# The factors of the x rows travel as a ninth column of the running sums

## What is computed

```python
def rms_norm(x, g):
    y = xf * lax.rsqrt(jnp.mean(xf * xf, axis=-1, keepdims=True) + EPS)
    return (y * g.astype(jnp.float32)).astype(x.dtype)

h = rms_norm(x, norm1_g)
proj = h @ w_in.astype(h.dtype)
...
a_cs = jnp.cumsum(a_dt, axis=-1)
seg = a_cs[..., :, None] - a_cs[..., None, :]
decay = jnp.where(mask, jnp.exp(jnp.where(mask, seg, 0.0)), 0.0)
```

## Time and profile before

| | us |
|---|---|
| median of 3 runs | 2737.02 |
| the runs | 2734.02, 2737.02, 2743.93 |
| the profiled execution | 2734.35 |
| its span, first to last instruction | 2732.5 |

### The profile page before, as it was taken

The page is one execution under the profiler, slowest core; times in us unless marked ns, Lnnn a source line. Parts: engine busy times, 40 slices in busy tenths (PEclk is TensorE's granted clock), DMA queues, the critical chain, the costliest instruction groups (busy, mean ns, idle before and its releaser), DMA issues.

```text
span 2732.5 us, 38705 instructions
## 1 busy us (share of the span) xinstructions
PE 2691.0 (98%) x11487; PEld 1741.9 (64%) x11487; DVE 2123.4 (78%) x6313; ACT 1415.0 (52%) x3262; POOL 703.6 (26%) x1278
## 2 busy tenths in 40 slices
PE   8999999999999999999999999999999999999996
PEld 6777677767776777777776777675444444444442
DVE  5777777677777767767767777776899999999997
ACT  2455544454445445554445444543666666666664
POOL 1021111211121112111211112112344444444444
PEclk9999999999999999999999999999999999999998
DMA  8212111121112111211122111237887777767654
GB/s 326 95 63 75 65 47 47 64 77 47 47 47 79 61 47 47 78 63 47 47 70 71 47 47 47 77 124 270 339 298 254 260 257 271 271 247 277 241 201 141
DMA packets 97589, 360.59 MB, mean 132 GB/s; under 512 B 29873, under 2 KB 31538, under 8 KB 87378
## 3 DMA queue, kind: packets, MB, share of 16 engines
q1 hardware_dynamic: 48850, 236.13, 24.5%
q0 software_dynamic: 48528, 121.90, 12.2%
HBM read 284.20 MB, written 121.46 MB: 148 GB/s over the span
## 4 chain that ended last, share of the span: by engine, by line
PE 95%; DMA 2%; DVE 2%; issue 1%; SPq 0%; POOL 0%; ACT 0%; POOLq 0%; DVEq 0%
PE PB L372 25%; PE PB L1761 20%; PE PB L383 17%; PE PB L460 12%; PE SS L1778 5%; PE TB L1778 5%; PE YB L460 4%; PE YB L414 2%; PE SS L423 1%; DMA arena<-in_w_in 1%; PE SS L427 1%; PE TB L436 1%; PE MB L405 1%; DVE xc L835 0%; DMA xc<-h_rows,bc 0%
## 5 line engine op out<-in xcount | busy, mean ns | idle before, releaser
L372 PE MATMUL PB<-arena,hT 128*128 128x512 f32 (+2 forms) x2112 | 726.6, 498 | 2.7 <-DVE x_res L955 1.5
L372 PEld LDWEIGHTS PB<-arena,hT 128*128 128x128 f32 x2112 | 396.6, 191 | 271.0 <-issue 222.9
L1761 PE MATMUL PB<-arena,hT 128*128 (+1 forms) x1280 | 562.5, 592 | 0.0
L383 PE MATMUL PB<-hT,arena 128*128 128x128 f32 x4224 | 486.5, 276 | 4.6 <-DVE arena L1171 4.6
L383 PEld LDWEIGHTS PB<-hT,arena 128*128 128x128 f32 x4224 | 481.1, 192 | 8.5 <-issue 4.8
L1761 PEld LDWEIGHTS PB<-arena,hT 128*128 128x128 f32 x1280 | 243.0, 190 | 304.8 <-issue 304.7
L460 PE MATMUL PB<-arena,tT 128*128 128x274 f32 (+1 forms) x1056 | 358.0, 493 | 0.3 <-ACT tT L646 0.3
L1208 POOL TENSOR_SCALAR rs<-sq 128x2 f32<-128x2 f32 (+1 forms) x66 | 12.6, 191 | 1207.0 <-ACT h L762 887.3
L1490 DVE STREAM_TRANSPOSE xdt<-gv 32x64 f32<-32x64 f32 x1232 | 290.5, 236 | 18.5
L460 PEld LDWEIGHTS PB<-arena,tT 128*128 128x128 f32 x1056 | 195.4, 190 | 139.9 <-issue 120.6
L835 DVE SCALAR_TENSOR_TENSOR xc<-xT,cols,xc 128x128 f32<-128x128 f32 x792 | 216.8, 347 | 3.5
(11 more groups left out here) (294 smaller groups left out, 3897.6 us busy)
## 6 DMA issues: line engine op xcount, KB each, us to landing
arena<-in_w_expert SPq DMA_DIRECT2D x32, 2048.0 KB, 8.3
arena<-in_w_expert SPq DMA_DIRECT2D x32, 1024.0 KB, 5.6
h_rows<-h SPq DMA_DIRECT2D x34, 512.0 KB, 6.0
x_in<-in_x_rows SPq DMA_DIRECT2D x33, 512.0 KB, 4.4
hT<-in_x_cols SPq DMA_DIRECT2D x33, 512.0 KB, 3.5
x_res<-in_x_rows SPq DMA_DIRECT2D x33, 512.0 KB, 3.5
dec<-running_sums SPq DMA_DIRECT2D x33, 512.0 KB, 3.6
x_rows<-x_res SPq DMA_DIRECT2D x33, 512.0 KB, 5.3
```

The source lines that it names most:

```text
L372: mm = nc.tensor.matmul(out, hT[u][:, k, :], w_group(name)[:, k, :], start=k == 0, stop=k == KD - 1)
L383: mm = nc.tensor.matmul(PB[b][:, c * P:(c + 1) * P], w_block(name, c)[:, k, :], hT[u][:, k, :], start=k == 0, stop=k == KD - 1)
L1761: mm = nc.tensor.matmul(PB[u][:, :], hT[u][:, k, :], arena[:, bass.ds(slot + k * 2 * DE, 2 * DE)], start=k == 0, stop=k == KD - 1)
```

## The change

The store of the running sums gets a ninth column in front, holding the x factor of the next tile: `e_in` becomes a part of `xr_e_in`, whose first column `xr` is where GpSimd writes the factor. The table in DRAM has nine numbers a row instead of eight, and the load spreads 1152 numbers to every partition instead of 1024 (`spread`). From tile 2 on, VectorE multiplies x by the spread column (step 9) instead of the bank in PSUM; tiles 0 and 1 still use the transposition. The decays are the other eight columns of `spread`, so that each of them is now read and written at a step of nine elements. SyncE's store also waits for the factor, and GpSimd, before it overwrites the factor, for an earlier store.

```diff
-        sums_d = nc.dram_tensor("running_sums", [P, H], F32).ap()
+        sums_d = nc.dram_tensor("running_sums", [P, 1 + H], F32).ap()
...
-        dec = sb("dec", [P, P * H])
-        dec_t = dec[:, :].rearrange("p (t h) -> p t h", h=H)
-        dec_h = dec[:, :].rearrange("p (t h) -> p h t", h=H)
+        spread = sb("spread", [P, P * (1 + H)])
+        x_factors = spread[:, :].rearrange("p (t h) -> p h t", h=1 + H)[:, 0:1, :]
+        dec_t = spread[:, :].rearrange("p (t h) -> p t h", h=1 + H)[:, :, 1:]
+        dec_h = spread[:, :].rearrange("p (t h) -> p h t", h=1 + H)[:, 1:, :]
...
-        e_in = sb("e_in", [P, 3 * H])
+        xr_e_in = sb("xr_e_in", [P, 1 + 3 * H])
+        xr, e_in = xr_e_in[:, 0:1], xr_e_in[:, 1:]
...
-            if tn.next2:
-                pe_spread(pe, i + 2, TB[0], [("ycat_hi", i + 1)])
...
-            nc.scalar.activation(dec[:, :], dec[:, :], ACT.Exp).then_inc(s["decay_ready"], 1)
+            nc.scalar.activation(dec_t, dec_t, ACT.Exp).then_inc(s["decay_ready"], 1)
...
         def dve_scale_x(dve, t, j, u):
-            dve.wait_ge(s["rbc_full"], t + 1)
             dve.wait_ge(xt_loaded[u], 16 * (j + 1))
-            V.tensor_tensor(hT[u][:, :, :], hT[u][:, :, :], TB[0][:, 0:1, :].broadcast_to([P, KD, P]), ALU.mult).then_inc(s["x_scaled"], 1)
+            if t < 2:
+                dve.wait_ge(s["rbc_full"], t + 1)
+                factors = TB[0][:, 0:1, :]
+            else:
+                dve.wait_ge(sums_spread, 16 * t)
+                factors = x_factors
+            V.tensor_tensor(hT[u][:, :, :], hT[u][:, :, :], factors.broadcast_to([P, KD, P]), ALU.mult).then_inc(s["x_scaled"], 1)
...
             after(pool, s["xi_ready"], t)
+            if t > 1:
+                pool.wait_ge(s["rbc_full"], 2)
+                pool.wait_ge(sums_stored, 16 * (t - 1))
...
             sp.wait_ge(s["acs_out"], t + 1)
-            sp.dma_start(sums_d, e_in[:, 0:H]).then_inc(sums_stored, 16)
+            sp.wait_ge(s["xr_ready"], min(t + 2, NT))
+            sp.dma_start(sums_d, xr_e_in[:, 0:1 + H]).then_inc(sums_stored, 16)
             sp.wait_ge(sums_stored, 16 * (t + 1))
             after(sp, s["ydiag_done"], t)
-            sp.dma_start(dec[:, :], sums_d.rearrange("(a t) h -> a (t h)", a=1).broadcast_to([P, H * P])).then_inc(sums_spread, 16)
+            sp.dma_start(spread[:, :], sums_d.rearrange("(a t) h -> a (t h)", a=1).broadcast_to([P, (1 + H) * P])).then_inc(sums_spread, 16)
...
-        g_buf = [flat(xc[:, :, :]), dec[:, :], x_in[1][:, :], x_in[0][:, :]]
+        g_buf = [flat(xc[:, :, :]), spread[:, 0:D], x_in[1][:, :], x_in[0][:, :]]
```

More of the change, by code:

```diff
@@ L391, in pe_spread @@
                 pe.wait_ge(s[sm], v)
-            nc.tensor.transpose(bank[:, 0, :], rs[:, 0:1].broadcast_to([P, P]), ident).then_inc(s["rbc_full"], 1)
+            nc.tensor.transpose(bank[:, 0, :], xr.broadcast_to([P, P]), ident).then_inc(s["rbc_full"], 1)
         def pe_front_sums(pe, t):
@@ L675, in act_front @@
             act.wait_ge(s["state_ready"], t + 1)
-            nc.scalar.activation(e_out[:, :], e_in[:, :], ACT.Exp).then_inc(s["eout_ready"], 1)
+            nc.scalar.activation(e_out[:, :], e_in, ACT.Exp).then_inc(s["eout_ready"], 1)
             act.wait_ge(s["seg_done"], t + 1)
-            nc.scalar.activation(dec[:, :], dec[:, :], ACT.Exp).then_inc(s["decay_ready"], 1)
+            nc.scalar.activation(dec_t, dec_t, ACT.Exp).then_inc(s["decay_ready"], 1)
         def act_xa(act, t):
@@ L1244, in pool_x_root @@
             after(pool, s["xi_ready"], t)
+            if t > 1:
+                pool.wait_ge(s["rbc_full"], 2)
+                pool.wait_ge(sums_stored, 16 * (t - 1))
             st.link(g.tensor_scalar(rs[:, 5:6], sq[:, 0:1], 1.0 / D, EPS, ALU.mult, ALU.add))
-            g.tensor_tensor(rs[:, 0:1], rs[:, 5:6], neg_half[:, 0:1], ALU.pow).then_inc(s["xr_ready"], 1)
+            g.tensor_tensor(xr, rs[:, 5:6], neg_half[:, 0:1], ALU.pow).then_inc(s["xr_ready"], 1)
             pool.wait_ge(s["xr_ready"], t + 1)
-            g.tensor_tensor(rinv[:, u:u + 1], rs[:, 5:6], rs[:, 0:1], ALU.mult).then_inc(s["xi_ready"], 1)
+            g.tensor_tensor(rinv[:, u:u + 1], rs[:, 5:6], xr, ALU.mult).then_inc(s["xi_ready"], 1)
         def pool_v(pool, st, t):
```

## The result

| | before | after |
|---|---|---|
| median of 8 runs, us | 2736.68 (2734.02 to 2743.93) | 2746.47 (2745.45 to 2749.38) |
| ratio to before | | 1.0034, 95% interval 1.0024 to 1.0045 |
| profiled execution (its span), us | 2734.35 (2732.5) | 2748.44 (2746.6) |

The kernel became 0.34% slower. The time lies in the range given and within the half per cent called "same", but a gain of 1 us was forecast and 9.8 us were lost: the sign was wrong, and rival C, with a chance of 0.23, is what happened.

A forecast was written before the change was run, and what follows sets the result against it. TensorE, busy 98% of the span, was taken to bound the kernel. 3.4 us from the transpositions, less 2.2 in turns 0 and 20 and 0.2 in thinly covered even turns, gave 1.0 us gained: 2736.0, range 2729 to 2749.

The forecast's parts named there:

- rival C: VectorE's addition at L955 bounds even turns, holding TensorE's next projection: 2760 with doubled surcharge, 2748 with later store; chance 0.23.
- What bounds the kernel: TensorE, busy 98% of the span; VectorE, at 78%, matters only once late enough to hold TensorE.
- D: Delay of VectorE's tail per turn, forecast 0.97 us; at 1.07 gain and loss cancel against the covers, TensorE's slack for L955.
- The scaling at 1.98 us: VectorE's L1044, reading factors from SBUF at 36 bytes: 0.77 us above its 1214 ns, by the surcharge of L889's strided read.
- the rival of a free step: L1044 on VectorE keeps its 1.21 us, covers hold: 2.8 us gained, 2734.2; chance 0.20.
- The 36-byte step: VectorE's L864 and L889, from 32 to 36 bytes: unchanged at 399 and 1076 ns; bounds 0.8 us less, 1.2 more.
- The load's growth: Spreading load (L1318) from 512 to 576 KB: 0.26 us at most, 0.2 taken, not hidden from VectorE.
- The new waits on GpSimd and SyncE: Store waiting for the next tile's factor, GpSimd for the previous turn's store: both cost nothing.
- "Larger transfers", the store at nothing: Store (L1315) rows from 32 to 36 bytes, same 128 pieces: nothing taken; bounds 0 and 1.6 us.
- one D for all turns, and a mean of the covers: Same D in each turn, set against covers: even turns 1.18 us in the mean (0.99 to 1.35), odd 1.9.
- turn 0 at D + 0.11: Turns 0 and 20, without cover, lose D plus TensorE's 0.11 us earlier arrival each: 2.2 us together.
- 3.4 us for the transpositions: TensorE's stream: 31 transpositions removed at 0.11 us each, gaining 3.4 us; upper end 8.4.

The follow-up runs named there:

- run 3: The kernel before with only its spreading load enlarged to 576 KB, store unchanged: 2735.83 beside 2737.20, ratio 0.9995.
- Run 9: The change with the decay products moved behind the first addition of x2 in turn 0 alone: 2739.46 beside 2735.66, ratio 1.0013.
- runs 5 and 6: The change, then the kernel before, each with VectorE's decay products moved behind the scaling and first addition of x2: 2731.20 and 2733.84, both beside 2736.11.
- run 1: The kernel before, with ScalarE copying the factor row into SBUF at a 32-byte step and the scaling reading it there: 2740.91 beside 2736.45, ratio 1.0018.
- runs 10 to 12: Factors by their own store: the change with a dense block, 2885.58; the kernel before without transposition from tile 2, own 64-KB load, 3004.32; and run 12.
- run 12: The change with factors stored as a dense block, that small store issued ahead of the load of x_res: 2922.83, ratio 1.0681.
- runs 2, 3 and 9: The first: the change with the transposition kept and used by the scaling, ninth column unread, 2738.64 beside 2736.45; the others: run 3 and Run 9.
- run 7: The change with ScalarE packing the factors into a dense row that the scaling reads: 2736.07 beside 2736.11, ratio 0.9999.
- run 4: The change with the transposition put back on TensorE, its result unread: 2745.03 beside 2737.20, ratio 1.0034.

## Why the prediction was wrong, step by step

**Right.** What bounds the kernel, and the place of rival C: the next projection's wait for the first L955 in the even turns, decided at a tail later by D = 1.07 us. The scaling at 1.98 us, priced by L889's surcharge, measured 1985 ns; the rival of a free step fell with it. The 36-byte step cost the other lines nothing. The Trainium skill (SBUF — State Buffer, Door 1: The DMA port swizzle) has every access pay that leaves a 16-byte line, which 32 and 36 bytes both do; the trace agrees with 1076 and 1073 ns. The load's growth was 0.2 as predicted (run 3: 0.17). The new waits on GpSimd and SyncE held nothing: the store is issued 3.49 us after the sums' matmul in both kernels.

**Wrong: "Larger transfers", the store at nothing.** Its 36-byte rows brought the median landing from 1.4 to 1.6 us. From the store's issue to the load's it is 1.54 us in the mean before and 1.80 after, from there to L860 3.70 and 4.00: 0.55 together, where 0.2 was taken; most of what was missing, 0.26, is the store's. D was 0.77 + 0.55 = 1.32 us, past the point of 1.07. The term was sized at its lower end for want of a row, with a margin of a tenth of a us to the point from which C decides.

**Wrong: one D for all turns, and a mean of the covers.** By the prediction's own arithmetic D = 1.32 costs 3.4 us net: 14 x (1.43 - 1.18) = 3.5 in the even turns, 2.9 in turns 0 and 20, 0.4 in turn 1 (an odd turn with a cover of 1.01, which the prediction put with the 1.9 of the others), less 3.4. But the time from the store to VectorE spread from 5.0 to 8.0 us over the turns, and from 4.8 to 6.4 before. When D is as large as the covers, a late turn loses its whole excess and an early one gives nothing back. Each turn's cover taken with each of the 30 measured differences of the transfers of turns 1 to 30, and turn 0 with its own, the mean loss comes out at about 7 us net: an estimate, made after the result. Each turn taken with its own transfers gives 7.4, and the trace shows 7.8 by turn 30 (11.2, less 2.8 for the clock in turn 0 and the 0.5 from before it).

**Wrong: turn 0 at D + 0.11.** The wait grew by 1.9 us, as its transfers were 1.07 later and not 0.2, and the granted clock after it, which the prediction did not think of, cost the profiled execution 2.8 more. The 7 of above, which holds the wait, and this 2.8 make the 9.8 of the medians, but that they meet so well is in part luck: the 2.8 are read from one execution, 2 us above the median of its kernel, and no other execution of it was traced. Of the 14.1 us between the two profiled executions 11.2 are lost by turn 30 and the other 2.9 in the slow stretch at the end of phase 1. Run 9 confirms turn 0's part within its interval.

**Half right: 3.4 us for the transpositions.** Each is 0.11 us on TensorE, and runs 5 and 6 give 3.5 us for all by their traces where TensorE sets the pace. But the gain was counted in full although half of the turns came to be paced by VectorE, and there most of it is waited away.

**Open.** Why the two transfers spread more from turn to turn is not settled, nor that the change makes them: run 1, with the transfers of before, spreads from 4.8 to 8.1 us, and run 3, with the larger load alone, from 4.9 to 7.0. What they cost in an execution is thus in part chance. How often the lower clock behind turn 0 falls in the changed kernel's executions is not known. Whether the two parts cost more together than their sum is not shown.

## To carry to other kernels

Hold an added delay against the thinnest cover, turn by turn, and against the spread of the transfers in front of it: as soon as the delay is about as large as the cover, variation is a loss in itself, and much of what the bound engine saves elsewhere is waited away. A few bytes more per row of a store on that chain need a price. Where a second engine comes near to setting the pace, look first whether it can do earlier what the bound engine waits for: moving two instructions behind the addition was worth 2.3 us without the change and nearly 15 with it (9.8 us slower became 4.9 faster), and made the change pay.

## What the runs showed of the hardware

A store in pieces of 4 bytes is slow out of all proportion to its size: 128 of them land in 8 to 12 us (runs 10 to 12), and the 512-KB load of x_res behind them in run 12 takes 10.3 us instead of 3.5, while 128 pieces of 32 or 36 bytes land in 1.4 and 1.6.

A single wait of TensorE can cost more than its length. Turn 0's first projection took 3.64 us to the next product in the kernel before and in runs 2, 3 and 9 (waits of 1.49, 1.84, 1.65 and 1.44 us ahead of it), 5.32 in run 1 (2.25 us, granted clock 0.79 over 127 to 135 us), 5.23 in run 7 (2.38 us, 0.80), 5.16 in run 4 (3.13 us, 0.79) and 6.46 after the change (3.38 us). The length of the wait does not set the cost: run 4 waited nearly as long as the change and its projection took 1.3 us less. And a wait is not needed just before: at the end of phase 1 the clock fell to 0.50 over 6.8 us in the trace of the change, in an unbroken stream of matmuls.
